# Rows of a mixture-of-experts stage gathered in quarters and turned on the vector engine, with other pieces, buffers and times of the weight loads

## What is computed

```python
h = rmsnorm(x, norm2_g) * (1.0 + scale2) + shift2
...
hid = jnp.einsum('nd,edf->nef', xt, exp_w13)
a, bgl = jnp.split(hid, 2, axis=-1)
act = jax.nn.silu(a) * bgl * gate[:, :, None]
out = jnp.einsum('nef,efd->nd', act, exp_w2)
```

## Time and profile before

| what | us |
|---|---|
| median of 3 runs | 566.37 |
| lowest and highest of them | 565.17, 568.79 |
| the profiled execution | 567.81 |
| its span (first to last instruction) | 566.1 |

### The profile page before, as it was taken

How to read it: one execution, slowest core, us unless ns; L and a number is a source line. 1 busy time by engine, 2 the same in 40 slices (tenths; PEclk the granted TensorE clock), 3 DMA queues, 4 the chain that set the end, 5 groups by cost and what they waited for, 6 DMA issues and landing times.

```text
span 566.1 us, 7601 instructions
## 1 busy us (share of the span) xinstructions
PE 515.8 (91%) x2906; PEld 260.7 (46%) x2906; DVE 288.0 (51%) x629; ACT 193.4 (34%) x356; POOL 90.2 (16%) x101
## 2 busy tenths in 40 slices
PE   3899999999999999999999999947999999979970
PEld 2445545554444566556545555533434443323320
DVE  4422755949420584211255455465666666655571
ACT  6322279992511220334512121121000333451531
POOL 3000000000530230000000000003023344442343
PEclk9999999999999999999999999967999999999995
DMA  8997646105580940620006390568899999998521
GB/s 327 387 269 228 194 158 214 37 10 168 195 296 7 339 158 2 195 87 1 1 0 221 137 349 36 223 223 302 339 361 403 413 402 370 389 371 349 227 64 66
DMA packets 62327, 120.53 MB, mean 213 GB/s; under 512 B 12033, under 2 KB 29778, under 8 KB 60242
## 3 DMA queue, kind: packets, MB, share of 16 engines
q1 hardware_dynamic: 53656, 104.23, 51.6%
q0 software_dynamic: 8496, 15.75, 7.7%
q10 hardware_dynamic: 138, 0.04, 0.0%
HBM read 112.36 MB, written 22.84 MB: 239 GB/s over the span
## 4 chain that ended last, share of the span: by engine, by line
PE 54%; DMA 5%; DVE 4%; ACT 2%; issue 1%; SPq 0%; POOL 0%; POOLq 0%; ACTq 0%; DVEq 0%
PE ps L1482 12%; PE ps L1195 11%; PE ms L1573 10%; PE ms L1569 5%; PE ps L1604 4%; DMA wring<-in_exp_w_dram 3%; PE ps L1600 2%; PE ps L1546 2%; PE ms L1455 1%; DMA sg<-in_state_gla_dram 1%; DMA mixT<-h_rows,slot_tok 1%; PE ps L1422 1%; PE ps L1412 1%; PE ps L1365 1%; PE ps L1584 1%
## 5 line engine op out<-in xcount | busy, mean ns | idle before, releaser
L1195 PE MATMUL ps<-r,wring 128*128 128x512 f32 (+1 forms) x512 | 143.5, 436 | 1.5 <-ACT mixT L983 0.9
L1195 PEld LDWEIGHTS ps<-r,wring 128*128 128x128 f32 x512 | 78.9, 191 | 67.3 <-issue 66.9
L1482 PE MATMUL ps<-wring,mixT 128*128 128x512 f32 x160 | 72.3, 598 | 0.3 <-DVE mixT L1967 0.3
L1573 PE MATMUL ms<-wring,tmp 128*32 128x512 f32 x288 | 67.4, 603 | 0.0
L760 POOL DMA_INDIRECT mixT<-h_rows,slot_tok x13 | 16.8, 1294 | 181.4 <-DVE slot_tok L2129 172.0
L1482 PEld LDWEIGHTS ps<-wring,mixT 128*128 128x128 f32 x160 | 29.2, 190 | 31.2 <-issue 31.2
L1269 PE MATMUL ps<-wring,r 128*128 128x512 f32 x80 | 35.6, 598 | 0.4 <-issue 0.4
L1129 ACT ACTIVATE tmp<-ms 128x256 f32<-128x256 f32 x13 | 5.0, 384 | 82.1 <-PE ms L1573 53.4
L1604 PE MATMUL ps<-wring,gd 128*32 128x512 f32 x144 | 32.5, 592 | 0.0
L1573 PE MATMUL ms<-r,tmp 128*32 128x512 f32 x144 | 24.0, 648 | 3.4 <-DMA wring<-in_exp_w_dram 3.4
L1102 ACT ACTIVATE gd<-xres 128x512 f32<-128x512 f32 x10 | 6.3, 630 | 56.7 <-DVE xres L2006 56.7
(11 more groups left out here) (366 smaller groups left out, 819.8 us busy)
## 6 DMA issues: line engine op xcount, KB each, us to landing
wring<-in_ada_w_dram SPq DMA_DIRECT2D x12, 2048.0 KB, 11.3
wring<-in_exp_w_dram SPq DMA_DIRECT2D x7, 2048.0 KB, 16.4
wring<-in_exp_w_dram SPq DMA_DIRECT2D x10, 1024.0 KB, 7.9
wring<-in_w_in_dram SPq DMA_DIRECT2D x16, 512.0 KB, 4.7
r<-in_exp_w_dram SPq DMA_DIRECT2D x4, 2048.0 KB, 15.4
tmp<-in_exp_w_dram SPq DMA_DIRECT2D x4, 2048.0 KB, 18.1
wring<-in_w_out_dram SPq DMA_DIRECT2D x2, 2048.0 KB, 12.3
vtok<-in_exp_w_dram SPq DMA_DIRECT2D x4, 1024.0 KB, 14.3
```

Source lines behind the costliest of these rows:

```text
L1195: i = mm(d, lhsT, r, start=first, stop=last)
L1482: i = mm(product(f"mx{t}")[:, half * 512:(half + 1) * 512], mixT[:, k, t * P:(t + 1) * P], w[:, k, :], start=(k == 0), stop=(k == KD - 1))
L1573: i = mm(ms[r:r + 32, b, :], xgT[:, b, k, r:r + 32], w[:, k, :], start=(k == 0), stop=(k == KD - 1), skip_group_check=True)
```

## The change

1. The normalised rows are stored in another order of columns, as four quarters of 256, so that column blocks of 32 can be turned one by one. normed_rows writes a row in four instructions, and scaled_rows writes to a buffer of its own.
2. For blocks 3 to 12 POOL gathers each block in four indirect transfers of 128 rows of 1 KB, each quarter to its own row number, and DVE turns the rows in blocks of 32x32 from SBUF to SBUF. turn_x on PE is gone there. Blocks 0 to 2 still gather whole rows and are turned on PE, in products of 32 columns. The row numbers of the quarters are made by DVE and spread over the partitions by PE (spread_rows); POOL waits for them before the gather for block 3.
3. A first-weights load brings 16 KB in one piece to each partition instead of 4 KB pieces.
4. The second weights have a fifth buffer, in two transfers of 512 KB, and their loads stand one block earlier in SP's queue. Loads n = 3 and 4 stand earlier still. The final gain is loaded before the stage.
5. Nine products whose result is not used (keep_going) stand on PE before rank and after table of the last tile.

```diff
         def first_weights(e):
-            return exp_w13[0, bass.ds(e, 1)].rearrange("a (c p j) f -> p (a c) (j f)", p=P, j=2)
+            return exp_w13[0, bass.ds(e, 1)].rearrange("z (p k) f -> p (z k) f", p=P)
...
+        e2_steps = [[w[:, k, :] for k in range(DC)] for w in e2] + [[qk[:, 0:D], mtmp]]
...
-        fing = tmp[:, 4 * N:4 * N + D]
+        fing = r1[:, W_WORDS:W_WORDS + D]
...
+        load2_slot = [0, 1, 2, 3, 4, 0, 2, 1, 3, 4, 0, 2, 1, 3, 0, 4]
+        freed2_by = [None] * 5 + [0, 1, 2, 2, 3, 4, 5, 6, 7, 8, 9]
...
             def load2(n, e):
                 w = exp_w2[0, bass.ds(e, 1)].rearrange("a (p k) f -> p (a k) f", p=P)
-                sp.dma_start(e2[load_slot[n]], w).then_inc(e2_in[load_slot[n]], 16)
+                if load2_slot[n] < 4:
+                    sp.dma_start(e2[load2_slot[n]], w).then_inc(e2_in[load2_slot[n]], 16)
+                else:
+                    for k in range(DC):
+                        sp.dma_start(e2_steps[4][k], w[:, k, :]).then_inc(e2_in[4], 16)
...
+            load2(3, first[3])
             sp.wait_ge(gx_in[0], 16)
             sp.wait_ge(logits_ready, NT)
...
             load13(3, first[3])
-            load2(3, first[3])
-            sp.wait_ge(h2_ready, NT)
-            sp.dma_start(fing, final_g.rearrange("(a n) -> a n", a=1).to_broadcast([P, D])).then_inc(fg_in, 16)
...
+                if n == 4:
+                    load2(n, e)
+                sp.wait_ge(hid, freed_by[n] + 1)
+                load13(n, e)
                 if n > 4:
-                    sp.wait_ge(y_done, 2 * (freed_by[n - 1] + 1))
-                    load2(n - 1, before_it)
-                before_it = e
+                    sp.wait_ge(y_done, 2 * (freed2_by[n] + 1))
+                    load2(n, e)
...
+            def gather_pieces(u):
+                b = u % 3
+                if u < 2 * W1:
+                    pool.wait_ge(x_turned, u - 2)
+                else:
+                    pool.wait_ge(x_taken, u - 2)
+                for g in range(QR):
+                    pool.indirect_dma_start(gx[:, b, SEG * g:SEG * g + SEG], None, h2_d.rearrange("n (i f) -> (n i) f", i=QR),
+                                            rows_at(piece_row[:, g, block_cols[u] - NG:block_cols[u] - NG + 1]),
+                                            bounds_check=QR * N - 1, oob_is_err=False).then_inc(gx_in[b], 16)
...
-            pool.wait_ge(routed, 2)
-            gather(3)
+            pool.wait_ge(routed, 4)
+            gather_pieces(3)
             for u in range(NB):
                 if u + 4 < NB:
-                    gather(u + 4)
+                    gather_pieces(u + 4)
...
+            def keep_going(n):
+                for _ in range(n):
+                    mm(ps[:, 2, 0:3 * P], ident[:, :], sg0[:, 0:3, :].rearrange("p g v -> p (g v)"), start=True, stop=True,
+                       skip_group_check=True)
...
                 for k in range(KD):
-                    i = nc.tensor.transpose(ps[:, 0, k * P:(k + 1) * P], step_of(gx[:, u % 3, :], k), ident[:, :])
+                    for r in range(QR):
+                        i = mm(ps[32 * r:32 * r + 32, 0, k * P:(k + 1) * P], piece_of(gx[:, u % 3, :], r, k), ident[:, :],
+                               start=True, stop=True, skip_group_check=True)
...
+            def spread_rows():
+                pe.wait_ge(routed, 3)
+                for g in range(QR):
+                    for r in range(0, P, 32):
+                        i = mm(ps[r:r + 32, 1, g * (NE - NG):(g + 1) * (NE - NG)], ident[:, 32 * g:32 * g + 32],
+                               piece_tok[:, :], start=True, stop=True, skip_group_check=True)
+                i.then_inc(tables, 1)
...
             turn_x(1)
+            spread_rows()
             gates_by_place()
...
-                if u + 2 < NB:
+                if u + 2 < W1:
                     turn_x(u + 2)
...
-                chain(tt_(h2[:, t % 2, cols], xres[:, t, cols], rows[seq][1][:, cols], ALU.mult))
+                chain(tt_(mtmp[:, cols], xres[:, t, cols], rows[seq][1][:, cols], ALU.mult))
...
-                stt(h2[:, t % 2, :], h2[:, t % 2, :], rt[:, 2, t:t + 1], rows[0 if t < ST else 1][2], ALU.mult, ALU.add).then_inc(h2_ready, 1)
+                for i in range(QR):
+                    n = stt(in_pieces(h2[:, t % 2, :], i), in_order(mtmp, i), rt[:, 2, t:t + 1],
+                            in_order(rows[0 if t < ST else 1][2], i), ALU.mult, ALU.add)
+                n.then_inc(h2_ready, 1)
...
             def take_x(u):
-                dve.wait_ge(x_turned, u + 1)
                 if u >= 2:
                     dve.wait_ge(hid, u - 1)
-                V.tensor_copy(xgT[:, u % 2, :, :].rearrange("p k n -> p (k n)"), ps[:, 0, :]).then_inc(x_taken, 1)
+                if u < W1:
+                    dve.wait_ge(x_turned, u + 1)
+                    V.tensor_copy(xgT[:, u % 2, :, :].rearrange("p k n -> p (k n)"), ps[:, 0, :]).then_inc(x_taken, 1)
+                else:
+                    dve.wait_ge(gx_in[u % 3], 16 * (QR * (u // 3) + 1))
+                    V.transpose(xgT[:, u % 2, :, :].rearrange("p k (g n) -> p g k n", g=QR),
+                                gx[:, u % 3, :].rearrange("p (g k a) -> p g k a", g=QR, k=KD)).then_inc(x_taken, 1)
```

More of the change, by code:

```diff
@@ L134, in hybrid_step, with piece_of, in_pieces, in_order @@
         e13 = [w.rearrange("p (k f) -> p k f", k=KD) for w in e13]
-        def pairs(w):
-            return w.rearrange("p (c j) f -> p c (j f)", j=2)
         def first_weights(e):
-            return exp_w13[0, bass.ds(e, 1)].rearrange("a (c p j) f -> p (a c) (j f)", p=P, j=2)
-        def step_of(rows, k):
-            return rows.rearrange("p (c n j) -> p c j n", n=P, j=2)[:, k // 2, k % 2, :]
+            return exp_w13[0, bass.ds(e, 1)].rearrange("z (p k) f -> p (z k) f", p=P)
+        QR = P // 32
+        SEG = D // QR
+        def piece_of(rows, i, k):
+            return rows[:, SEG * i + 32 * k:SEG * i + 32 * k + 32]
+        def in_pieces(row, i):
+            return row[:, SEG * i:SEG * i + SEG].rearrange("p (k a) -> p a k", k=KD)
+        def in_order(row, i):
+            return row[:, SEG * i:SEG * i + SEG].rearrange("p (a k) -> p a k", k=KD)
         mix_flat = mixT[:, :, :].rearrange("p k n -> p (k n)")
@@ L477, in hybrid_step @@
         e13_in = [sem(f"e13_in{i}") for i in range(4)]
-        e2_in = [sem(f"e2_in{i}") for i in range(4)]
+        e2_in = [sem(f"e2_in{i}") for i in range(5)]
         e13_head = sem("e13_head")
@@ L1576, in hidden, with second_weights @@
                     i.then_inc(hid, 1)
+            def second_weights(n):
+                return (16 if load2_slot[n] < 4 else 16 * DC) * load2_slot[:n + 1].count(load2_slot[n])
             def turn_a(u):
@@ L1590, in output @@
                 own, shared = block_loads(u)
-                pe.wait_ge(e2_in[load_slot[own]], 16 * (own // 4 + 1))
+                pe.wait_ge(e2_in[load2_slot[own]], second_weights(own))
                 if shared is not None:
-                    pe.wait_ge(e2_in[load_slot[shared]], 16 * (shared // 4 + 1))
+                    pe.wait_ge(e2_in[load2_slot[shared]], second_weights(shared))
                 for half in range(2):
@@ L1632, in _ @@
                         for k in range(KD):
-                            m = nc.tensor.transpose(ps[:, 0, k * P:(k + 1) * P], step_of(gx[:, 0, :], k), ident[:, :])
+                            for r in range(QR):
+                                m = mm(ps[32 * r:32 * r + 32, 0, k * P:(k + 1) * P], piece_of(gx[:, 0, :], r, k), ident[:, :],
+                                       start=True, stop=True, skip_group_check=True)
                         m.then_inc(ov["xT"], 1)
@@ L2018, in normed_rows @@
                 link(V.reciprocal(rt[:, 2, t:t + 1], rt[:, 1, t:t + 1]))
-                stt(h2[:, t % 2, :], h2[:, t % 2, :], rt[:, 2, t:t + 1], rows[0 if t < ST else 1][2], ALU.mult, ALU.add).then_inc(h2_ready, 1)
+                if t >= 2:
+                    dve.wait_ge(h2_out[t % 2], 16 * (t // 2))
+                for i in range(QR):
+                    n = stt(in_pieces(h2[:, t % 2, :], i), in_order(mtmp, i), rt[:, 2, t:t + 1],
+                            in_order(rows[0 if t < ST else 1][2], i), ALU.mult, ALU.add)
+                n.then_inc(h2_ready, 1)
             def by_group(ap):
@@ L2188, in _ @@
             fill_shared(3, tok_place, tok_row).then_inc(routed, 1)
+            dve.wait_ge(routed, 2)
+            settle()
+            ts_(piece_tok, slot_tok[:, NG:NE], -float(N), None, ALU.add).then_inc(routed, 1)
             oh = r16[:, 0:2, :, :]
```

42 lines of the change are left out of this document (23 added, 19 removed).

## The result

The changed kernel takes 570.4 us (median of 20 runs, 566.62 to 572.23) against 567.65 us for the kernel before on the same chips (20 runs). The ratio is 1.0048, with a 95% interval of 1.0028 to 1.0068: half a per cent slower, inside the 1% that was called no change, where 561.3 had been forecast. The profiled execution has a span of 570.0 us against 566.1.

The account below looks back on a forecast made before the run. PE was taken to bound the kernel, with weights 3.4 us behind at one block; -9.6 + 3.4 + (4.5 - 3.4) = -5.1 us on the profiled 567.81 gave 562.7, or 561.3 against the runs' median; range 550 to 575.

Parts of the forecast that it names:

- PE's saving: On PE, blocks 3 to 12 lose their turn of gathered rows: 10 x 0.96 = -9.6 us.
- its price in front: Work added on PE and ahead of it, at the first blocks: +3.4 us, with ends +0.7 and +9.
- the spread: Spreading the row numbers on PE, between turn 1 and the gate products: 32 records of 12 columns, 1.4 us.
- The turn on DVE: From block 3 on, DVE turns rows in 1.22 to 3 us, fitting its free time: priced at nothing.
- The sooner loads: Ahead of load n=13: early second weights and final gain -4.0, fifth buffer -2.6, second weights n=12 in front +2.7 us.
- The step that failed: At block 10, load n=13 lands at 505.0, so PE waits 4.5 us for weights in place of 3.4.
- the 16 KB pieces: First weights in pieces of 16 KB instead of 4 may run better: 0 to -3, taken as -1 us.
- The third rival: In the full stage, gathers starve behind 16 KB weight packets and DVE's turn waits: 573 us (570 to 577), chance 0.20.
- the +2 us that stood for rows of 1 KB: Nine gathers in rows of 1 KB ahead of load n=13 delay it: nothing to +5, taken as +2 us.
- The sum: Per block of the expert stage, weights and POOL's rows need 13.0 us of all DMA engines; PE's period falls to 10.8.
- the first rival: All transfers come in time, so block 10's weight wait and its low clock go: -11.3, 555.1 us (551 to 559), chance 0.28.
- the one for the first rival: The sign, in the expert stage, that all transfers come in time: no wait for weights at all.

Follow-up runs that it names:

- The fourth experiment: The changed kernel with second weights in four buffers and loaded at the times of before, the rest kept: 573.01 us, 1.0113 to the kernel before.
- the second experiment: The kernel before with first weights in pieces of 16 KB, its turn reading the gathered rows with another stride: 566.04 us, 1.0004.

## Why the prediction was wrong

**PE's saving was right, its price in front too high.** The ten turns left the chain: 10.53 us a block. The start cost +0.2 us up to block 3 where I had +3.4, an error that worked in the change's favour. Four pieces of the timeline show it:

```profile
387.21 0.63 PE L1611 MATMUL ms<-r,tmp 128*32 128x512 f32 x3
...
394.11 1.93 PE L1583 MATMUL ps<-ident,mixT 128*32 128x128 f32 x64
395.85 0.46 PE L1653 MATMUL ps<-tmp,ident 128*32 128x12 f32 x32
...
398.59 3.64 PE L1611 MATMUL ms<-wring,tmp 128*32 128x512 f32 x32
```

The turn of block 1 takes 1.74 us to the next instruction (1.79 forecast), the spread about 0.4 (1.4 forecast), block 0's product 6.9 (7.14 forecast), and block 1's product starts at 398.59 for 398.47 before. The rest, in the start up to the first turn, cost nothing.

**The turn on DVE** was rightly placed at nothing as far as DVE's own time goes. By its group it is as long as the copy it replaces (1224 ns):

```profile
L2308 DVE STREAM_TRANSPOSE tmp<-mixT 128x1024 f32<-128x1024 f32 x10 | 12.5, 1245 | 7.1 <-DMA mixT<-h_rows,piece_row 6.9
```

**The sooner loads** were to bring one load 3.9 us sooner. The fourth experiment has 3.7 us of time, with an interval that reaches from next to nothing to twice that, and one of the terms stayed in place there. That the numbers are alike shows little.

**The step that failed** is the one on the weights: "So it lands at 507.9 - 4.0 - 2.6 + 2.7 + 2 - 1 = 505.0, a wait of 4.5 us". I worked out the limit of the DMA engines at one load alone, and gave the 16 KB pieces -1 us, as a matter of rate. The rate came out (417 GB/s from 430 to 470 us, 408 before), but the sum has no term for what the pieces do to POOL's queue: waits for put-backs, residual rows and give-outs stood at nothing, without a reason. They are what PE stood for, 12.7 us through DVE where the sum has one wait of 4.5 for weights. Load n = 13 was issued at 489.79, as late as before, since PE's stall at 484 held SP back; it landed at 500.4, and nobody waited for it. With 4 KB pieces, in four transfers, the wait at this place was 10.5 us. Long packets took the time from POOL's queue: a put-back that landed after 8 to 11 us with 4 KB needs up to 24 with 16 KB. The Trainium skill's page "DMA: Bandwidth & Descriptors" ("Queues, rings and completion order") says that an engine drains a packet of one queue before it turns to the next; the landings agree with it.

In the span the parts are -9.6 for the turns, +0.2 for the start, 12.7 - 4.8 = +7.9 for the waits, 4.3 - 1.8 = +2.5 for the clock behind them and +2.4 for the tail, +3.4 in all; the span grew by 3.9, and the last 0.5 is not placed.

**The third rival** had this mechanism, and looked at the wrong transfer. Gathers have 22 us of lead, and DVE waited for them 6.9 us in all. The put-back, the residual rows behind it and the give-outs have hardly any, and they stand behind the same packets. The rival asked when a gather is late; the question was which transfer of that queue has the least lead. (With whole rows at 16 KB it was a gather after all: 27.2 us, with PE waiting 6.56.) Its count of packets was wrong too. The page of the changed kernel has:

```profile
q1 hardware_dynamic: 48072, 104.23, 50.5%
q0 software_dynamic: 8976, 15.75, 8.0%
```

For q0 that is 480 more than before, 30 per engine. Ten gathers of 9 packets per engine have become forty, so a quarter is 3 packets per engine and the four of a block 12, not 36. With 128 rows over 16 engines a packet must then hold several rows of 1 KB. (The 27 and 32 packets in the expectations of two runs go by the same wrong count, and no run isolates the +2 us that stood for rows of 1 KB.) At 438 to 443 us, where their landings can be read, the last of four quarters landed 21.5 us after the first was issued, where the rival had 28.

**The sum** I had in hand and set aside: 13.0 us of DMA work a block against a period of 10.8. I put it as an argument against the first rival. Read as a forecast it says that, with the bytes unchanged, the gain on PE comes back as a wait somewhere. The runs agree with that, though no run measures the bound itself. From 380 to 530 us the DMA share is 0.92 to 0.95 before, in the changed kernel, with 4 KB, with 8 KB and with whole rows, and 0.87 to 0.91 with fewer bytes. Three packet lengths put the waits at different places (12.7 us through DVE, 8.3 us through DVE, 10.5 us at the weights), and the times lie within 0.9%. A gain beyond 0.5% came only with fewer bytes: 557.9, where the rival in which everything is in time had 555.1 without the longer tail. The length of the packets still mattered with fewer bytes (563.88 with 4 KB), so the sum is not the whole account.

**The tail** was taken as unchanged and is 2.4 us longer: of the 3.9 us by which the span grew, 1.5 lie ahead of the last put-back's issue (558.67 before, 560.18 now) and 2.4 behind it. Of the signs that I had named, the one for the first rival came true, no wait for weights at all, and the time of that rival did not come with it: I had named no sign for late put-backs.

Not settled: the tail; how the loss would divide with other lengths for the second weights; and what part POOL's full row has in it. With quarters POOL issues eight transfers a block, some 1.3 us each with the gap, which fills the block's 10.5 us, so that after a wait of 12.55 us it has no room to catch up; with whole rows it issues five. No run separates this from the packets. A load order that fills the gap at 400 to 410 (DMA share 0.59) would need more buffers, and was not tried.

## What to carry to other kernels

When two resources are both full, add up the work of the second per period before pricing a saving on the first; if the sum exceeds the new period, expect the saving to come back as a wait, once what was loaded ahead is used up, and ask where. When packets of one queue are made longer, look up the lead of every transfer in the queues beside it, beginning with the shortest: here the gathers had 22 us and the round trip of residual rows through DRAM hardly any. Price what stands behind each of them. A reordered or lengthened row of transfers is best judged by landing times, since the waits only name the last in the chain.

## What the runs showed of the hardware

- Longer pieces in one queue delayed the transfers of the other: put-backs of 0.5 MB at most, issued between 424 and 510 us in the changed kernel and its two versions with shorter pieces, landed after 8 to 11 us with weights in 4 KB pieces, 9 to 24 with 8 KB and 11 to 24 with 16 KB. In the kernel before, 16 KB alone took them from 8 or 9 us to 11 to 20.
- A piece of 16 KB counts as one packet (q1 has 47640 packets in the second experiment against 53656 before, 376 fewer per engine for 16 loads), and an indirect transfer of 128 rows of 1 KB counts as 3 packets per engine, one of 128 rows of 4 KB as 9.
- With nine unused products on PE the granted clock was 0.93 between 380 and 390 us (0.67 to 0.94 over the kernels that have them), where it was 0.56 before and 0.50 without them.
- The 16 products of the spread (32 records of 12 columns) took about 0.4 us, some 12 ns a record; the bounds had been 0.4 and 3.4 us.
- A turn of 128x1024 numbers in blocks of 32x32 from SBUF to SBUF took DVE 1245 ns, and a copy of as many numbers from PSUM 1224 ns.
- Between the last transfer's issue and the end of the span the kernels with quarters need 9.8 us and the others 7.4. No instruction in the profile explains it, and shortening a branch that is not taken did not change it.
